# A two-layer hybrid attention block: shift, scale and gate computed on four 32-column tiles of the array, all in the first layer's front half

## The reference, cut to what matters

```
m = silu(cvec) @ ada_w[l] + ada_b[l]            # (1024) @ (1024, 6144)
shift1, scale1, gate1, shift2, scale2, gate2 = six rows of 1024
h = rms_norm(x, norm1_g[l]) * (1 + scale1) + shift1
proj = h @ w_in[l]                              # GLA, convolution and attention parts
mix = [gla, convolution, attention] @ w_out[l]
x = x + gate1 * mix
h2 = rms_norm(x, norm2_g[l]) * (1 + scale2) + shift2
x = x + gate2 * peer(h2, ...)                   # 8 heads x 16 experts for every token
```

## Time and profile before

| | us |
|---|---|
| median of three runs | 4717.09 |
| the profiled execution's own time | 4720.62 |
| its span, first to last instruction | 4718.80 |
| layer 0: front, project, attention | 74.91, 176.08, 229.07 |
| layer 0: peer | 1781.41 |
| layer 1: front, project, attention | 25.64, 176.81, 143.17 |
| layer 1: peer, with the last stores | 1697.36 |

### The profile page before, as it was taken

How to read it: one execution, slowest core, us unless ns; L and a number is a source line. 1 busy time by engine, 2 the same in 40 slices (tenths; PEclk the granted TensorE clock), 3 DMA queues, 4 the chain that set the end, 5 groups by cost and what they waited for, 6 DMA issues and landing times.

```text
span 4718.8 us, 50122 instructions
## 1 busy us (share of the span) xinstructions
PE 3170.2 (67%) x17114; PEld 1368.6 (29%) x17114; DVE 2801.8 (59%) x6305; ACT 962.5 (20%) x2405; POOL 2691.6 (57%) x2759
## 2 busy tenths in 40 slices
PE   7999775666666666665558987666655666666655
PEld 3466531222222222221114565312212212212211
DVE  1612547666666666666635355576676776666763
ACT  1122211112112122122111151112122212212211
POOL 1900016667667667677756400277777777777775
PEclk8999587787888778788779995877778767777778
DMA  5113039999999999999981102299999999999998
GB/s 183 37 57 102 32 119 368 399 404 402 398 396 402 398 396 401 398 397 406 400 343 38 42 15 79 102 409 409 409 406 404 405 407 403 400 410 407 403 407 343
DMA packets 512225, 1455.45 MB, mean 308 GB/s; under 512 B 52896, under 2 KB 171108, under 8 KB 511844
## 3 DMA queue, kind: packets, MB, share of 16 engines
q0 software_dynamic: 368640, 1342.34, 72.0%
q1 hardware_dynamic: 143336, 109.94, 7.5%
HBM read 1448.86 MB, written 3.24 MB: 308 GB/s over the span
## 4 chain that ended last, share of the span: by engine, by line
PE 31%; DMA 23%; DVE 17%; POOL 14%; issue 12%; ACT 2%; DVEq 1%; SPq 0%; ACTq 0%; POOLq 0%
PE ps L538 30%; DMA arena<-in_peer_u,expert_rows 11%; DMA arena<-in_peer_v,expert_rows 11%; POOL arena L513 7%; POOL arena L521 7%; DVE arena L1374 6%; PE ps L642 1%; DVE arena L1291 1%; DVE arena L1322 1%; DVE top_indices L1321 1%; DVE arena L1356 1%; DVE arena L1353 1%; DVE chosen_pair L1358 1%; DVE top_values L1324 0%; DVE best_positions L1321 0%
## 5 line engine op out<-in xcount | busy, mean ns | idle before, releaser
L538 PE MATMUL ps<-arena 64*64 64x512 f32 (+5 forms) x14768 | 2779.0, 688 | 1372.8 <-issue 1089.2
L1374 DVE CUSTOM_DVE_ANT_0 arena<-arena,ps 128x1024 f32<-128x1024 f32 x1280 | 1527.2, 1218 | 923.4 <-DMA arena<-in_peer_u,expert_rows 921.1
L538 PEld LDWEIGHTS ps<-arena 64*64 64x64 f32 (+2 forms) x14768 | 1142.6, 181 | 2947.0 <-issue 2834.5
L513 POOL DMA_INDIRECT arena<-in_peer_u,expert_rows x1280 | 1212.2, 947 | 767.4 <-issue 313.0
L521 POOL DMA_INDIRECT arena<-in_peer_v,expert_rows x1280 | 1206.7, 943 | 432.8 <-issue 347.5
L1123 ACT ACTIVATE arena<-constants,expert_weight 128x64 f32<-128x64 f32 x1280 | 382.1, 339 | 1375.7 <-PE ps L538 1352.0
L500 POOL MEMSET arena<- 128x5632 f32 x2 | 9.6, 4792 | 408.3 <-ACTq L256 408.3
L1219 DVE TENSOR_REDUCE score_max<-ps 128x1 f32<-128x640 f32 (+1 forms) x80 | 57.4, 718 | 305.7 <-PE ps L538 305.7
L538 PE MATMUL ps<-arena,cond_silu 128*2 128x128 f32 (+1 forms) x1344 | 201.0, 308 | 18.8 <-DMA arena<-in_ada_w 11.5
L493 POOL TENSOR_SCALAR arena<-arena,vec_columns 128x512 f32<-128x512 f32 x120 | 153.1, 1287 | 10.2 <-issue 10.2
L538 PEld LDWEIGHTS ps<-arena,cond_silu 128*2 128x2 f32 x1344 | 114.5, 90 | 149.9 <-issue 103.9
(11 more groups left out here) (157 smaller groups left out, 1776.4 us busy)
## 6 DMA issues: line engine op xcount, KB each, us to landing
arena<-in_ada_w SPq DMA_DIRECT2D x80, 512.0 KB
arena<-in_peer_u,expert_rows POOLq DMA_INDIRECT x1280
arena<-in_peer_v,expert_rows POOLq DMA_INDIRECT x1280
arena<-in_w_in SPq DMA_DIRECT2D x32, 512.0 KB, 4.1
arena<-in_ada_w SPq DMA_DIRECT2D x4, 2048.0 KB, 17.8
arena<-in_w_out SPq DMA_DIRECT2D x4, 2048.0 KB, 7.9
arena<-in_peer_wq SPq DMA_DIRECT2D x2, 4096.0 KB, 17.7
peer_modulation<-modulation_rows SPq DMA_DIRECT2D x4, 1536.0 KB, 12.0
```

The costliest lines, as they stand in the source:

```text
L513: pool.indirect_dma_start(UR[:, k % RING, :], None, u_rows, bass.IndirectOffsetOnAxis(ap=rows[:, g % LIVE, k:k + 1], axis=0))\
L538: return pe.matmul(out, lhsT, rhs, start=start, stop=stop)
L1374: dve.tensor_tensor_reduce(out=UR[:, k % RING, :], in0=UR[:, k % RING, :], in1=pair(1), scale=1.0, scalar=0.0, op0=ALU.mult, op1=ALU.add, ...
```

## The change

All 128 columns of a PE pass are used: the silu vectors are padded with zeros to 32 columns, and four matmuls in a row write to four PSUM partition groups (0, 32, 64, 96), each with another 128 columns of `ada_w`. A piece is now 512 columns (`mod_chunk`, 32 calls and four for the bias), loaded as two halves of 256 columns. Layer 0's shift1 and scale1 are four such pieces in `start`; the other 20 (8 of layer 0, 12 of layer 1) are 13 behind the projection blocks 3 to 15 of layer 0 and 7 in its attention. `peer` has none.

Shift1 and scale1 no longer go through memory. PE turns the evacuated rows with a matmul into columns (`turn_rows`, 8 columns wide), and they are applied to the transposed tokens, where a channel is a partition: half of each tile's evacuation on ACT, half on DVE. DVE's two passes before the transpose become one (times `rstd`). Layer 0's token tiles 0 and 1 are transposed before the modulation is there, and the tokens and constants are loaded ahead of the slabs. The gain is loaded as columns, in pieces of one number.

```
-        cond_s = sb("cond_silu", [P, KT, 2])
+        cond_s = sb("cond_silu", [P, KT, 32])
...
+        CHUNKS = [(0, 512 * n) for n in range(WIDE, 12)] + [(1, 512 * n) for n in range(12)]
...
+        IN_PROJECT = NB - FIRST_MOD
+
+        def in_attention(i):
+
+            n = IN_PROJECT + (i - 2) // 4
+            return n if i >= 2 and i % 4 == 2 and n < NC else None
...
+            def load_chunk(n):
+
+                l, c0 = CHUNKS[n]
                 aw = ada_w[l].rearrange("(p k) n -> p k n", p=P)
-                sp.dma_start(ada_slab[slot][:, 0:KT, :], aw[:, :, bass.ds(c0, P)]).then_inc(slab_in[slot], 16)
-                sp.dma_start(ada_slab[slot][0:1, KT, :], ada_b[l:l + 1, bass.ds(c0, P)]).then_inc(slab_in[slot], 16)
-
-            def store_rows(l, done, c0):
-
-                sp.wait_ge(S["m_row_done"], done)
-                sp.dma_start(scratch[l, :, bass.ds(c0, P)], m_chunk).then_inc(S["mod_out"], 16)
+                for half in range(2):
+                    c = bass.ds(c0 + 256 * half, 256)
+                    sp.dma_start(ada_slab[half][:, 0:KT, :], aw[:, :, c]).then_inc(slab_in, 16)
+                    sp.dma_start(ada_slab[half][0:1, KT, :], ada_b[l:l + 1, c]).then_inc(slab_in, 16)
+
+            def chunk_done(n):
+
+                sp.wait_ge(S["m_ps"], WIDE + n + 1)
+                if n + 1 < NC:
+                    load_chunk(n + 1)
+                if n not in COLS:
+                    l, c0 = CHUNKS[n]
+                    sp.wait_ge(S["m_row_done"], WIDE + n + 1)
+                    for j in range(4):
+                        sp.dma_start(scratch[l, :, bass.ds(c0 + P * j, P)], m_chunk[32 * j:32 * j + 2, :])\
+                            .then_inc(S["mod_out"], 16)
...
+                sp.dma_start(X[:, 0:NT_S, :], x_sample[0].rearrange("(t p) d -> p t d", p=P)).then_inc(S["x_in"], 16)
+                sp.dma_start(X[:, NT_S, :], x_prompt[0]).then_inc(S["x_in"], 16)
+                sp.dma_start(CST[:, :], consts).then_inc(S["const_in"], 16)
...
-                sp.wait_ge(S["m_row_done"], WIDE)
-                sp.dma_start(scratch[0, :, 0:2 * D], m_row).then_inc(S["mod_out"], 16)
-                load_vectors(0)
-                sp.dma_start(gain1, norm1_g[0:1, :].to_broadcast([P, D])).then_inc(S["gain1_in"], 16)
-                sp.wait_ge(S["mod_out"], 16)
-                load_rows(0, MOD1[:, 0:2], 0, 2, "mod_in")
+                    if n == 0:
+                        sp.dma_start(ada_bias, ada_b[0:1, 0:2 * D]).then_inc(S["adab_in"], 16)
+                for l in range(DEPTH):
+                    sp.dma_start(gain_col[:, l, :], norm1_g[l].rearrange("(k p) -> p k", p=P),
+                                 allow_slow_non_contiguous=True).then_inc(S["gain1_in"], 16)
                 for b in range(WRING):
                     load_block(0, b)
+                sp.wait_ge(S["m_ps"], WIDE)
+                load_vectors(0)
...
+                    if l == 0 and b == 1:
+                        load_chunk(0)
+                    if l == 0 and in_project(b) is not None:
+                        chunk_done(in_project(b))
...
-                sp.wait_ge(S["res_done"], NT * (l + 1))
-                for n in range(2):
-                    load_slab(l + 1, P * n, n)
-                with sp.Fori(0, M_BLOCKS // 2 - 1) as i:
-                    for j in range(2):
-                        store_rows(l + 1, M_EXPERTS + 2 * i + j + 1, i * (2 * P) + P * j)
-                        load_slab(l + 1, i * (2 * P) + P * (j + 2), j)
-                for n in (M_BLOCKS - 2, M_BLOCKS - 1):
-                    store_rows(l + 1, M_EXPERTS + n + 1, P * n)
...
-                sp.wait_ge(S["mod_out"], 16 * (1 + LATE + M_BLOCKS))
-                sp.wait_ge(S["u_free"], TOPK * T * (l + 1))
-                load_rows(l + 1, MOD1[:, 0:2], 0, 2, "mod_in")
...
+                pe.wait_ge(S["const_in"], 16)
+                for t in range(2):
+                    h_transposes(0, t)
...
                     for k in range(KT):
-                        m = mm(PS[0:2, n % 2, :], cond_s[:, k, :], wide_slab[n][:, k, :], k == 0, k == KT - 1)
+                        for j in range(4):
+                            mm(PS[32 * j:32 * j + 32, 4 + n, 0:P], cond_s[:, k, :], wide_slab[n][:, k, P * j:P * j + P],
+                               k == 0, False)
+                    for j in range(4):
+                        m = mm(PS[32 * j:32 * j + 2, 4 + n, 0:P], CST[0:1, C_ONE:C_ONE + 2],
+                               ada_bias[:, 512 * n + P * j:512 * n + P * j + P], False, True)
                     m.then_inc(S["m_ps"], 1)
...
+                for n in range(WIDE):
+                    pe.wait_ge(S["m_row_done"], n + 1)
+                    turn_rows(m_first[:, n, :], 4 + n)
...
+            def turn_rows(rows_of, bank):
+
+                m = mm(PS[:, bank, 256:264].rearrange("p (j g) -> p j g", j=4), rows_of,
+                       ident.rearrange("p (j c) -> p j c", j=4)[:, :, 0:2])
+                m.then_inc(S["mc_ps"], 1)
...
+            def mod_chunk(bank, n):
+
+                pe.wait_ge(slab_in, 64 * (n + 1))
+                pe.wait_ge(S["m_row_done"], WIDE + n)
+                if n - 1 in COLS:
+                    turn_rows(m_chunk, bank)
+                    pe.wait_ge(S["mc_done"], n - COLS[0])
                 for k in range(KT):
-                    mm(PS[0:2, bank, 0:P], cond_s[:, k, :], ada_slab[slot][:, k, :], k == 0, False)
-                mm(PS[0:2, bank, 0:P], CST[0:1, C_ONE:C_ONE + 2], ada_slab[slot][0:1, KT, :], False, True)\
-                    .then_inc(S["m_ps"], 1)
+                    for j in range(4):
+                        mm(PS[32 * j:32 * j + 32, bank, 0:P], cond_s[:, k, :],
+                           ada_slab[j // 2][:, k, P * (j % 2):P * (j % 2) + P], k == 0, False)
+                for j in range(4):
+                    m = mm(PS[32 * j:32 * j + 2, bank, 0:P], CST[0:1, C_ONE:C_ONE + 2],
+                           ada_slab[j // 2][0:1, KT, P * (j % 2):P * (j % 2) + P], False, True)
+                m.then_inc(S["m_ps"], 1)
...
-                        if l == 0 and t < 4 and h < 6 and k in (4, 14):
-                            j = k // 10
-                            block = 12 * t + 2 * h + j
-                            mod_block(7, j, 32 * (LATE // 2 + block // 2 + 1), M_EXPERTS + block)
...
+            def mod_rows(bank, n):
+
+                if n - 1 in COLS:
+                    c = n - 1 - COLS[0]
+                    act.wait_ge(S["mc_ps"], WIDE + c + 1)
+                    act.activation(mod_col[:, 1, 4 * c:4 * c + 4, :],
+                                   PS[:, bank, 256:264].rearrange("p (j g) -> p j g", j=4), ACT.Copy)\
+                        .then_inc(S["mc_done"], 1)
+                act.wait_ge(S["m_ps"], WIDE + n + 1)
+                act.wait_ge(S["mod_out"], 64 * stored(n))
+                act.activation(m_chunk, PS[:, bank, 0:P], ACT.Copy).then_inc(S["m_row_done"], 1)
...
+                def h_out(t):
+                    act.wait_ge(S["mc_ready"], l + 1)
                     act.wait_ge(S["ht_ps"], NT * l + t + 1)
-                    act.activation(HT[:, :, P * t:P * t + P], pair(t % 2).rearrange("p (k n) -> p k n", k=KT),
-                                   ACT.Copy).then_inc(S["ht_ready"], 1)
+                    for k in range(KT // 2):
+                        c = mod_col[:, l, :, group_of(t)]
+                        m = act.activation(HT[:, k, P * t:P * t + P], pair(t % 2)[:, P * k:P * k + P], ACT.Identity,
+                                           bias=c[:, k:k + 1], scale=c[:, KT + k:KT + k + 1])
+                    m.then_inc(S["ht_act"], 1)
...
-                scale_gain(MOD1, gain1)
-                for t in range(NT):
+                def scaled(t):
                     if t >= 2:
                         dve.wait_ge(S["ht_ps"], NT * l + t - 1)
-                    g = group_of(t)
-                    st.link(stt(hbuf[:, t % 2, :], X[:, t, :], rstd[:, t:t + 1], MOD1[:, 1, g, :], ALU.mult, ALU.mult))
-                    tt(hbuf[:, t % 2, :], hbuf[:, t % 2, :], MOD1[:, 0, g, :], ALU.add).then_inc(S["h_ready"], 1)
+                    ts(hbuf[:, t % 2, :], X[:, t, :], rstd[:, t:t + 1], None, ALU.mult).then_inc(S["h_ready"], 1)
+
+                def h_out(t):
+                    dve.wait_ge(S["ht_ps"], NT * l + t + 1)
+                    c = mod_col[:, l, :, group_of(t)]
+                    for k in range(KT // 2, KT):
+                        m = ts(HT[:, k, P * t:P * t + P], pair(t % 2)[:, P * k:P * k + P], c[:, KT + k:KT + k + 1],
+                               c[:, k:k + 1], ALU.mult, ALU.add)
+                    m.then_inc(S["ht_dve"], 1)
...
+                        dve.wait_ge(S["m_ps"], n + 1)
+                        dve.tensor_copy(m_first[:, n, :], PS[:, 4 + n, 0:P]).then_inc(S["m_row_done"], 1)
+                    for n in range(WIDE):
+                        dve.wait_ge(S["mc_ps"], n + 1)
```

(35 more changed lines are left out.)

125 lines of the change are left out of this document (58 added, 67 removed).

## The result

The changed kernel takes 4561.31 us (median of four runs, 4553.52 to 4564.45) beside 4717.49 for the kernel before, measured with it: a ratio of 0.9666, 95% interval 0.9655 to 0.9678. The forecast was 4585. Its direction and its order of size are right, but the time came out 24 us lower: just under the forecast's own range (4562 to 4606) and at the low end of the wide one (4560 to 4632). The profiled execution took 4560.16 us, its span is 4558.4.

A forecast was written before the change was run, and what follows sets the result against it. PE was taken to bound project and attention, and full DMA the gather stretches of peer. Attention -67.7, peer -80.1, project +39.3, fronts -19 and -5 sum to -132.5 us: forecast 4585 us, own range 4562 to 4606, wide range 4560 to 4632.

The forecast's parts named there:

- PE bounds project and attention, and a piece's price decides there: Layer 0's project and attention: PE is the bound, so work put on it adds to the time, 2.6 us a piece.
- A piece of 2.6 us: Project and attention: 64 records on four column tiles take 1.95 us, plus 0.65 for bias calls and changes of shape.
- Project, +39.3: Layer 0's project: 13 pieces +33.8 us, turns +4.0, slab stalls +3, less 1.5 behind block 15.
- Layer 0's peer gains 80.1, at most 82: Layer 0's peer: dropping 48 blocks saves 80.1 us, the gather stretches' difference between layers (1399.11 against 1319.04); upper bound 82.
- The lower bound, 63 us by bytes at the mean rate: Layer 0's peer: the 48 blocks' 25.2 MB at the stretch's full DMA rate account for 63 us of gain.
- First front: Layer 0's start: projection begins near 56 us instead of 74.91, so -19 us; vectors land at 48, 0.9 added for queueing.
- Second front: Layer 1's start: two folds and five times two DVE passes give way to shorter work, -5 us (-8 to -1).
- pairs: Rival for the pieces: PE works on only two column tiles at a time, 4.7 us a piece, 4627 us; chance 0.12.
- open loads: Rival in project: next piece's loads don't fit behind a block, half open adds 61 us, 4646 us; chance 0.07.
- the slow one: Rival: packed calls run serially at half clock, 16.2 us a piece, 4857 us, slower than before; chance 0.04.
- serial: Pieces one by one at full clock, 8.1 us each, 4695 us; chance 0.04 together with a case under 4562.
- The better case: First front reaches 51 us and a piece 2.0: 4568 us, or 4565 with shorter second-front passes.

## Why the prediction was right and where not

- *PE bounds project and attention, and a piece's price decides there*: right. The change of order alone moved the time by 76 us, and taking the calls out by 18.
- *A piece of 2.6 us*: the mechanism was right (1.95 us for the records), the 0.65 around it too much: 2.26 in attention. That is 2.4 of the 3.7 us that attention came out lower. The other 1.3 is layer 1's attention, from which both prices are taken: 143.17 us in the one profile and 141.87 in the other, with the same code.
- *Project, +39.3*: a second step that was mis-sized; it measured 32.2. The slab stalls were 0.2 us where 3 were set. The rest of PE's work took 2.2 us less at its higher granted clock, which no term has. The remaining 2 are pieces and turns. The turns themselves were right: from a turn to its piece it is 3.8 us in all, 2.1 of them waiting, where 4 were set.
- *Layer 0's peer gains 80.1, at most 82*: the step that failed most, 8.9 us of the 27.9 between the two sums. It took layer 1's stretch for what layer 0's would be without blocks (4 to 5 us too long), and left out the 2 MB of rows (5 to 6 us at the end of the gathers) and the gain load. By parts, the stretch gave 85.4 us and the end up to the last gather 4.9, and the rest of the stage took 1.3 back. The bound of 82 stood on the same comparison, so the range had no room on that side: the 89.0 measured exceed it. The lower bound, 63 us by bytes at the mean rate, was also not a price of these loads.
- *First front*: right to about 1 us on the path (the columns came 2 us earlier, off the path), but by luck in one place: SP was held 12.4 us at the gain loads and 5.4 at the weight blocks, not the 0.9 added for queueing, and that ended 0.5 us before the fourth slab's piece.
- *Second front*: right; 1.4 us more, from the pass of 0.74 us less what the short operations took longer.
- *Layer 1 from project on*: 5.6 us that no term has. The kernel before without its blocks runs unchanged code there and took 2220.7 us (its span less the start of layer 1's first projection matmul) against 2224.6 before and 2219.0 after. Four profiles of the code of before have 2220.7 to 2224.6, nine of the changed code 2217.7 to 2221.8. So part of it is the spread between executions; whether the 3 us between the two means belong to the change stays open.
- *Rivals*: pairs, open loads and the slow one did not come. The pieces of 4.7 us (pairs) and 8.1 (serial) are 3.9 and 7.05 with more around them than the 0.65 of the forecast, and that is not worked out. The better case had only a faster front and piece in it, and nothing for peer, where more than half of the gain was.

## What to carry to other kernels

In a stage where the DMA engines are full, price a transfer by the time its packets take (its queue's share times the stretch), not by its bytes at the stage's rate: here that held for the slabs (85.3 us for 84.5) and nearly for the rows (5.1 for 5.9). List every load that a change removes, those at the stage's edges too. Before one layer is taken as the baseline of another, allow for their own difference, and give a gain's upper bound that much room. Before an issue that takes long on SP is put down to its own load, look at what still moves ahead of it. For narrow matmuls, let neighbours in the program write to different column tiles.

## What was not expected of the hardware

- Packets of 512 bytes moved at 290 GB/s of engine time beside gathers at 394; row loads of 3.8 KB a packet, on the same queue as the former, at about 410.
- Four 32-column tiles over 128 rows: 1.95 us for 64 records, 3.05 times the speed of one tile; two tiles 1.81 times.
- The same 4 KB load in pieces of four bytes held SP for 6.2 us behind slabs that were still moving and 1.8 behind weight blocks; three weight blocks of 0.5 MB took SP 5.4 us behind the gain loads and 2.5 without them there.
